# Low parts of three of 28 weight slots a unit made by accumulating DMAs from GpSimd instead of VectorE

## What is computed

```
h      = rmsnorm(x, norm_w[l])
proj   = h @ w_in[l]                    # 2048 x 22544: 14 blocks of 1024 columns, gates of four branches
y_a    = gated DeltaNet (conv, chunked WY form, 8 heads of 128)
y_b    = HGRN2 (chunkwise, 8 heads)
y_c    = S5 (diagonal complex SSM, GLU)
y_d    = retention with rotary positions (8 heads)
merged = sum over the branches of sigmoid(gate) * (y @ w_branch[l, branch])
x      = x + merged @ w_out[l]
```

## Time and profile before

| | us |
|---|---|
| median of 3 executions (2977.65 to 2981.5) | 2978.66 |
| the profiled execution | 2980.86 |
| its span, first to last instruction | 2979.0 |
| TensorE busy | 2919.3 (98%) |
| VectorE busy | 2072.9 (70%) |
| ScalarE busy | 1491.7 (50%) |
| GpSimd busy | 319.2 (11%) |

### The profile page before, as it was taken

One profiled execution on the slowest core, in us unless ns is written; L12 is line 12 of the kernel. 1 busy time (PEld: TensorE's weight loads), 2 busy tenths in 40 slices (PEclk: granted clock), 3 DMA queues, 4 the chain that ended last, 5 costly groups with the idle time before them and its releaser, 6 DMA issues.

```text
span 2979.0 us, 49428 instructions
## 1 busy us (share of the span) xinstructions
PE 2919.3 (98%) x19452; PEld 2664.7 (89%) x19452; DVE 2072.9 (70%) x3417; ACT 1491.7 (50%) x2209; POOL 319.2 (11%) x525
## 2 busy tenths in 40 slices
PE   7999999999999999999999999999999999999998
PEld 7899999999998888888899999999999988888887
DVE  7888787878776555555568887787788755545554
ACT  6455545554554444444555455545554644444443
POOL 3112022212200000000010221122120000000000
PEclk9999999999999999999999999999999999999999
DMA  6455555555556666665645555555555666666655
GB/s 169 124 148 147 151 147 152 147 149 146 150 166 194 195 191 196 193 193 183 195 115 142 147 152 153 149 146 146 151 144 146 178 195 192 194 193 193 195 179 168
DMA packets 614103, 492.34 MB, mean 165 GB/s; under 512 B 18544, under 2 KB 496560, under 8 KB 613488
## 3 DMA queue, kind: packets, MB, share of 16 engines
q1 hardware_dynamic: 606800, 483.44, 56.5%
q0 software_dynamic: 6688, 4.64, 0.7%
q10 hardware_dynamic: 384, 1.11, 0.1%
HBM read 487.02 MB, written 2.10 MB: 164 GB/s over the span
## 4 chain that ended last, share of the span: by engine, by line
PE 59%; issue 24%; DVE 10%; DVEq 6%; ACT 1%; DMA 0%; POOL 0%; ACTq 0%; POOLq 0%
PE PJ L1701 38%; PE S L1701 7%; PE GA L1701 4%; PE HA L1701 4%; PE RA L1701 3%; PE GB L1701 2%; DVE w_lo L1118 2%; DVEq L1306 2%; DVE region L1289 1%; DVE mix L1229 1%; DVEq L1521 1%; DVEq L1256 1%; DVEq L1285 1%; DVE work L1252 1%; DVE hkq L1304 1%
## 5 line engine op out<-in xcount | busy, mean ns | idle before, releaser
L1118 DVE TENSOR_TENSOR w_lo<-raw_w,w_hi 128x1024 fp32r<-128x1024 f32 x912 | 1115.9, 1225 | 697.3 <-ACT w_hi L573 671.9
L573 ACT ACTIVATE w_hi<-raw_w 128x1024 fp32r<-128x1024 f32 x912 | 964.2, 1060 | 784.8 <-PE PJ L1701 330.6
L1701 PE MATMUL PJ<-h_hi,w_hi 128*128 128x256 f32 x3584 | 1047.1, 292 | 0.0
L1701 PE MATMUL PJ<-h_hi,w_lo 128*128 128x256 f32 x3584 | 1014.6, 283 | 0.0
L1701 PE MATMUL PJ<-h_lo,w_hi 128*128 128x256 f32 x3584 | 1014.3, 283 | 0.0
L1701 PEld LDWEIGHTS PJ<-h_hi,w_hi 128*128 128x128 f32 x3584 | 687.2, 192 | 12.9 <-issue 12.6
L1701 PEld LDWEIGHTS PJ<-h_lo,w_hi 128*128 128x128 f32 x3584 | 687.6, 192 | 0.0
L1701 PEld LDWEIGHTS PJ<-h_hi,w_lo 128*128 128x128 f32 x3584 | 686.5, 192 | 0.0
L1701 PE MATMUL PJ<-w_hi,h_hi 128*128 128x512 f32 x640 | 249.2, 389 | 2.0 <-DVE h_lo L1610 2.0
L1701 PE MATMUL PJ<-w_hi,h_lo 128*128 128x512 f32 x640 | 249.0, 389 | 0.0
L1701 PE MATMUL PJ<-w_lo,h_hi 128*128 128x512 f32 x640 | 249.0, 389 | 0.0
(11 more groups left out here) (427 smaller groups left out, 4137.9 us busy)
## 6 DMA issues: line engine op xcount, KB each, us to landing
raw_w<-w_in SPq DMA_DIRECT2D x704, 512.0 KB, 3.7
raw_w<-w_branch SPq DMA_DIRECT2D x128, 512.0 KB, 4.3
raw_w<-w_out SPq DMA_DIRECT2D x64, 512.0 KB, 4.4
raw_w<-s_glu_w SPq DMA_DIRECT2D x16, 512.0 KB, 4.7
ret_decay<-c_ret POOLq DMA_DIRECT2D x16, 128.0 KB, 3.2
out<-x_tok SPq DMA_DIRECT2D x4, 512.0 KB, 4.0
x_tok<-x ACTq DMA_DIRECT2D x1, 1024.0 KB, 7.7
x_tok<-x SPq DMA_DIRECT2D x1, 1024.0 KB, 8.2
```

The costliest lines, as they stand in the source:

```text
L573: A_(w_hi[i % RING][:, :, :], raw_w[i % RING][:, :, :], ACT.Copy).then_inc(hi_ready, 1)
L1118: TT(w_lo[i % RING][:, :, :], raw_w[i % RING][:, :, :], w_hi[i % RING][:, :, :].bitcast(f32), ALU.subtract).then_inc(raw_used[i % RING], 1)
L1701: return nc.tensor.matmul(o, w, m, start=start, stop=stop)
```

## The change

In each unit the slots 18, 20 and 22 take another way. VectorE's ahead leaves them out. ScalarE writes two tiles for them: first w_lo = -raw_w, rounded to fp32r (the negated high part), then w_hi as before; a drain follows, and hi_ready is raised behind it. GpSimd, after its s5_matrices, waits for hi_ready of each of the three in turn, issues a DMA that adds raw_w onto w_lo (SBUF to SBUF, accum_op add), waits until it has landed, and then adds 1 to raw_used[i % 4] in VectorE's place.

```diff
@@ constants
 USES = HALVES // RING
+DMA_LOW = (18, 20, 22)
+LOW_PARTS = len(DMA_LOW)
@@ semaphores
-        hi_ready, split_used = sem("hi_ready"), sem("split_used")
+        hi_ready, split_used, low_landed = sem("hi_ready"), sem("split_used"), sem("low_landed")
@@ GpSimd, in the loop over units
                     if n1 < DEPTH * UNITS:
                         s5_matrices(n1)
+                    for j, i in enumerate(DMA_LOW):
+                        pool.wait_ge(hi_ready, l * SPLITS + u * HALVES + i + 1)
+                        pool.dma_start(w_lo[i % RING][:, :, :], raw_w[i % RING][:, :, :], accum_op=ALU.add).then_inc(
+                            low_landed, 16)
+                        pool.wait_ge(low_landed, 16 * ((n1 - 1) * LOW_PARTS + j + 1))
+                        pool.sem_inc(raw_used[i % RING], 1)
@@ ScalarE, in the loop over units
                     def ahead(i):
 
-                        split_hi(i + RING, s0, r0)
+                        if i + RING in DMA_LOW:
+                            act.wait_ge(split_used, s0 + (i + RING + 1))
+                            act.wait_ge(raw_full[i % RING], r0 * 16 + 16 * ((i + RING) // RING + 1))
+                            A_(w_lo[i % RING][:, :, :], raw_w[i % RING][:, :, :], ACT.Copy, scale=-1.0)
+                            A_(w_hi[i % RING][:, :, :], raw_w[i % RING][:, :, :], ACT.Copy)
+                            act.drain().then_inc(hi_ready, 1)
+                        else:
+                            split_hi(i + RING, s0, r0)
@@ VectorE, in the loop over units
                     def ahead(i):
 
-                        split_lo(i + RING, s0)
+                        if i + RING not in DMA_LOW:
+                            split_lo(i + RING, s0)
```

## The result

| | before | after |
|---|---|---|
| median, us | 2978.66 (2977.65 to 2981.5, 7 runs) | 2986.8 (2984.47 to 2990.5, 7 runs) |
| span of the profiled execution | 2979.0 | 2988.7 |

The change makes the kernel slower, by a quarter of a per cent: ratio 1.0026, 95% interval 1.0017 to 1.0035. The forecast was 2952.

The account below looks back on a forecast made before the run. TensorE, 98% busy, was taken as the bound, losing time only in waits on VectorE: HA 17.5, GA 4.8 and L1961 some 5 make 27 us, giving 2952 us. Its own range was 2946 to 2962, widened to 3010.

Parts of the forecast that it names:

- The bound, and what VectorE's relief is worth: TensorE is busy 98%; three subtractions a unit off VectorE win only TensorE's waits on it, 27 us in the run.
- The three waits named: TensorE's weight loads waiting behind VectorE's h_scores (21.5 us) and invert (4.8), and on L1961 (6.3).
- the four us that lie ahead of slot 18: Three HA waits of TensorE's weight loads, 4.0 us together, earlier in the unit and expected to stay.
- ScalarE: One more activation (1.06 us) and a drain (some 0.15) a slot fit ScalarE's idle time; nothing on the path.
- The chain on GpSimd, and where it starts to hurt: GpSimd's three transfers follow one another from 1777.2; slots 18, 20, 22 tolerate X up to 7.1, 7.2, 7.5.
- The limit for the gain: X of 7.8 us, at which all of the gain would be gone.
- 1777.2 + 3X: When slot 22's low part is ready after three chained transfers; compared with 1799.7, and with 1801.2 now.
- X: Time from GpSimd's issue of an addition to the moment that TensorE may go.
- I take X = 6.0: GpSimd's additions take 6.0 us each: near the middle of 4.6 and 6.4, plus half a microsecond for sharing.
- The rule weighed: An addition inside a DMA halves the rate, as two sources share one queue; it speaks for X of 6.4.
- Rival A: Slow transfers make GpSimd's chain the path at project(20) and project(22): 3003 us at X = 8.5; chance 0.25.
- the likeliest case: The forecast itself, with X of 6.0 and nothing new on the path: 2952 us, chance 0.59.

Follow-up runs that it names:

- e3: The changed kernel without the three additions, ScalarE itself adding to raw_used, so the low part stays the negated high part: 2948.14 us, 0.9896 of before.
- e4: The changed kernel with SyncE's load of slot 22 held until the addition of slot 20 has landed: 2972.97 us, one run.
- e9: The kernel of e2 with SyncE's load of slot 22 held until w_hi of slot 20 is ready, so loads 22 and 23 start with the addition: 2964.43 us, one run.
- e2: The changed kernel with only slot 20 taking the new way, one addition a unit: 2959.54 us, 0.9935 of before.
- e7: The changed kernel with only slots 18 and 22 taking the new way, two additions a unit: 2950.78 us, 0.9905 of before.
- e5: The changed kernel with a plain copy of raw_w onto w_lo in place of each addition: 2944.0 us, one run.
- e6: The changed kernel with SyncE issuing load 23 before 22 and 25 before 24: 2951.53 us, 0.9902 of before.
- e8: The changed kernel with slots 16, 19 and 22 taking the new way instead of 18, 20 and 22: 2951.59 us, 0.9906 of before.

## Why the prediction was wrong

- **The bound, and what VectorE's relief is worth: right.** 27 us by the sum, 30.4 by e3. The three waits named went, for the reason given, and the four us that lie ahead of slot 18 stayed. The waits that went came to 28.3 us in the changed kernel and 26.5 in e3; where the other 4 us of e3's gain are from isn't settled.
- **ScalarE: right.** The second activation and its drain are hidden (e3).
- **The chain on GpSimd, and where it starts to hurt: right in its build.** With the unit's own numbers it adds up: GpSimd starts at 1783.17, 6.87 us behind project(14)'s first weight load, 6.8 by the prediction. Then 5.67 to landing and 0.64 to the next issue, 9.23 and 0.57, 8.41 and 0.15 to project(22): 31.54 us behind project(14), where it was 30.84 before the change. The limit for the gain was a little off: by the prediction's own line, 1777.2 + 3X reaches 1801.2 at X = 8.0 and not at 7.8. The mean of 5.7, 8.4 and 8.7 is 7.6, and with half a microsecond of hand-over between the links, which I had left to X, it is 8.1, just beyond either.
- **The step that failed** is "I take X = 6.0, near the middle of 4.6 and 6.4 with half a microsecond for sharing", one value for all three transfers. For a transfer whose second load goes out half a microsecond ahead, and the first 3 us ahead, it is right (5.7). For the other two the sharing is not 0.5 us but 3.7 on top of the 4.6 that an addition takes alone (e4): its first packet moves 4.3 us after the issue instead of 1.5, and from there to the last packet it takes 3.7 instead of 2.8. A sum of work comes to the same: 1.8 us in which the engines do nothing for it, 2.8 us of engine time (both from e4), and 1.85 us for each of two raw loads beside it, the figure that the prediction itself had worked out from the earlier trace rows, make 8.3 (8.3 in e9, 8.4 and 8.7 in the changed kernel). That is a fit at one point and no law: with one load it would give 6.45, and 5.3 to 5.8 was measured where one load goes out 0.5 to 0.7 us ahead (slot 18, e2, slot 22 in e7). Why the addition's packets come so late when two loads start with it, no run shows.
- The reason for it stood in the prediction and wasn't followed up. It said that the load of 22 would wait for the landing of 18 and that 23 and 24 stand behind it, and asked only whether ScalarE would get them in time. It would. The question left out was what these loads run beside, once they are let go at the very moment at which the next addition starts.
- **The rule weighed**, that of the Trainium skill (Collectives: The Full Stack, "The bandwidth ceiling"), stands there for the reduce step of ring collectives, where two sources are read through one ring. For the engine time the traces here agree: 2.65 us for an addition against 1.42 for a copy (e5). In the landing it is only 0.8 us, and the loss of the change came from the additions' neighbours, not from their second read.
- **Rival A happened**, at the near edge of its price. It had a chance of 0.25, and the range up to 3010 covered 2986.8; the likeliest case was the wrong one. Its reasons, the unknown rate of the addition and the two reads, were not what made it true: an addition by itself takes 4.6 us.
- What stays open is the spread of a single landing, 8.1 to 9.8 us at slots 20 and 22 with the two loads beside at nearly the same distance. No run here tells what the slower ones met.

Of the versions that compute the whole low part, e6, e7 and e8 are the fastest and can't be told apart, at 2950.8 to 2951.6, just under 1% below before. e7 does it with two additions a unit and no change to the order of the loads.

## What to carry to other kernels

Before work is moved to a DMA, list what its completion lets go: a buffer freed at a landing starts the next load at that moment, and an engine that issues its loads in order adds those whose buffers were free already, so the traffic can bunch just where the next transfer of the chain begins. As a first bound, cost the transfer as its time alone plus the engine time of everything that starts beside it, and not as its own time plus a margin. Where one engine lags, one or two instructions taken off ahead of the wait bring most of the gain; here the first slot brought 23 of the 30 us and a second one (e7) 5 more.

## What the runs showed of the hardware

- An accumulating transfer of 512 KB within SBUF, issued by GpSimd, lands in 4.6 us (median of 16, e4) with no load beside it, of which the 16 DMA engines are busy some 2.8. With loads beside it as for slot 18, a plain copy takes them 1.42 us instead of 2.65 and lands 0.8 us sooner (e5).
- Transfers that start together don't share the engines evenly. In the unit shown the first load landed after 3.9 us as if alone, the second after 9.5 and the addition after 9.2, with 2 of its 144 packets moved in its first 4.4 us.
- The hand-over from a landing, through GpSimd's semaphore, to SyncE is short in this unit: 0.07 us lay between the landing of an addition and the issue of the load that it frees, while GpSimd itself needs 0.57 us from a landing to its next issue.
